# Gated delta rule in a three-way mixer: early preparation, a smaller last doubling, and query work moved later

## The reference, cut to what matters

```python
proj = rms_norm(h, norm_mix_pre[l]) @ w_in[l]
(aq, ak, av, cb, cc, cx, gq, gk, gv, ga, gb, gg) = jnp.split(proj, split_idx, axis=-1)
# delta rule, per head and chunk
rel = jnp.exp(jnp.where(causal, decay[..., :, None] - decay[..., None, :], -jnp.inf))
a = jnp.where(strict, jnp.einsum('bhnik,bhnjk->bhnij', k_beta, k) * rel, 0.0)
sol = lax.linalg.triangular_solve(eye + a, rhs, left_side=True, lower=True, unit_diagonal=True)
attn = jnp.where(causal, jnp.einsum('bhnik,bhnjk->bhnij', q, k) * rel, 0.0)
q_dec = q * jnp.exp(decay)[..., None]
def step(state, inp):
    v_new = u_i - jnp.einsum('bhck,bhkv->bhcv', w_i, state)
    o_i = einsum(q_i, state) + einsum(attn_i, v_new)
    state = state * cd_i[..., None, None] + jnp.einsum('bhck,bhcv->bhkv', k_i, v_new)
# then rms_norm(o, norm_w) * silu(gate), concatenated with the other two parts, @ w_out
```

## Time and profile before

| | us |
|---|---|
| median of 3 runs (2716.85 to 2727.89) | 2717.04 |
| the profiled execution | 2713.73 |
| its span, first to last instruction | 2711.9 |
| TensorE busy in the span | 2573.2 (95%) |
| VectorE busy | 1681.6 (62%) |
| ScalarE busy | 1136.8 (42%) |
| mean granted clock of TensorE | 0.976 |

### The profile page before, as it was taken

How to read it: one execution, slowest core, us unless ns; L and a number is a source line. 1 busy time by engine, 2 the same in 40 slices (tenths; PEclk the granted TensorE clock), 3 DMA queues, 4 the chain that set the end, 5 groups by cost and what they waited for, 6 DMA issues and landing times.

```text
span 2711.9 us, 34553 instructions
## 1 busy us (share of the span) xinstructions
PE 2573.2 (95%) x13186; PEld 2055.0 (76%) x13186; DVE 1681.6 (62%) x3253; ACT 1136.8 (42%) x2073; POOL 0.2 (0%) x4
## 2 busy tenths in 40 slices
PE   7998999899999999988999999999999999999897
PEld 5876879678888878668886788888876667787566
DVE  6756546455446776565564554468477676599664
ACT  4235444443232242454444433223345677232563
POOL 0000000000000000000000000000000000000000
PEclk9989999999999999899999999999899999999999
DMA  4310024123335622100331232375110000122221
GB/s 146 104 60 19 1 87 139 39 78 101 96 99 202 194 74 98 57 10 1 109 124 48 78 98 96 95 239 191 45 47 24 17 17 17 62 78 78 59 58 48
DMA packets 73507, 219.37 MB, mean 81 GB/s; under 512 B 21248, under 2 KB 21504, under 8 KB 72576
## 3 DMA queue, kind: packets, MB, share of 16 engines
q1 hardware_dynamic: 48384, 176.29, 20.1%
q10 hardware_dynamic: 24960, 40.87, 4.9%
HBM read 215.03 MB, written 2.10 MB: 80 GB/s over the span
## 4 chain that ended last, share of the span: by engine, by line
PE 80%; DVE 12%; ACT 5%; issue 2%; DMA 1%; ACTq 0%; DVEq 0%; SPq 0%
PE bank L575 20%; PE bank L576 19%; PE bank L577 19%; PE bank L842 4%; PE bank L806 4%; DVE c_y L2150 3%; PE bank L816 3%; DVE w_lo L541 2%; PE bank L1297 1%; PE bank L1305 1%; PE bank L606 1%; ACT w_hi L534 1%; PE bank L608 1%; PE bank L607 1%; PE bank L1243 1%
## 5 line engine op out<-in xcount | busy, mean ns | idle before, releaser
L575 PE MATMUL bank<-a_hi,w_hi 128*128 128x512 f32 (+1 forms) x1480 | 587.4, 397 | 25.4 <-DVE a_lo L712 16.0
L534 ACT ACTIVATE w_hi<-w_raw 128x1024 fp32r<-128x1024 f32 x334 | 353.0, 1060 | 570.3 <-PE bank L577 539.8
L576 PE MATMUL bank<-a_lo,w_hi 128*128 128x512 f32 (+1 forms) x1480 | 579.0, 391 | 0.0
L577 PE MATMUL bank<-a_hi,w_lo 128*128 128x512 f32 (+1 forms) x1480 | 579.0, 391 | 0.0
L541 DVE TENSOR_TENSOR w_lo<-w_raw,w_hi 128x1024 fp32r<-128x1024 f32 x334 | 407.7, 1223 | 232.8 <-ACT w_hi L534 232.1
L575 PEld LDWEIGHTS bank<-a_hi,w_hi 128*128 128x128 f32 (+1 forms) x1480 | 278.1, 188 | 97.3 <-issue 32.1
L576 PEld LDWEIGHTS bank<-a_lo,w_hi 128*128 128x128 f32 (+1 forms) x1480 | 278.0, 188 | 61.2 <-issue 3.0
L577 PEld LDWEIGHTS bank<-a_hi,w_lo 128*128 128x128 f32 (+1 forms) x1480 | 278.0, 188 | 60.8
L575 PE MATMUL bank<-b_hi,w_hi 128*128 128x512 f32 x704 | 258.4, 367 | 1.0 <-DVE w_lo L541 0.8
L576 PE MATMUL bank<-b_lo,w_hi 128*128 128x512 f32 x704 | 249.8, 355 | 0.0
L577 PE MATMUL bank<-b_hi,w_lo 128*128 128x512 f32 x704 | 248.3, 353 | 0.0
(11 more groups left out here) (399 smaller groups left out, 4019.6 us busy)
## 6 DMA issues: line engine op xcount, KB each, us to landing
w_raw<-w_tiles SPq DMA_DIRECT2D x334, 512.0 KB, 3.5
mod_raw<-mod_tiles ACTq DMA_DIRECT2D x48, 512.0 KB, 4.2
d_bias<-rpb_rows ACTq DMA_DIRECT2D x16, 224.0 KB, 4.5
hT<-xT ACTq DMA_DIRECT2D x4, 512.0 KB, 11.0
m_in<-memT ACTq DMA_DIRECT2D x2, 1024.0 KB, 4.7
mod_cond<-cond_rows ACTq DMA_DIRECT2D x2, 1024.0 KB, 6.2
out<-hT ACTq DMA_DIRECT2D x8, 256.0 KB, 2.6
ctx_sq<-ctxT ACTq DMA_DIRECT2D x1, 1024.0 KB, 7.7
```

Source lines behind the costliest of these rows:

```text
L534: act.activation(w_hi[:, t % SPLIT, :], w_raw[:, t % RAW, :], ACT.Copy).then_inc(sem("w_rounded"), 1)
L575: pe.matmul(o, wh, hi[:, k, :n], start=k == 0, stop=False)
L576: pe.matmul(o, wh, lo[:, k, :n], start=False, stop=False)
L577: mm = pe.matmul(o, wl, hi[:, k, :n], start=False, stop=k == kc - 1)
```

## The change

It does the following; no arithmetic of the result is left out.
- Preparation is interleaved with the input jobs: l2 sums and the turning of a and b after job ak0, two swaps after aq1, two swaps and the decay sums after cg0, the values' turning after cx0. VectorE's and ScalarE's parts are set one or more jobs behind (`in_between_*`). Each square follows the SiLU it needs. The loading of the count mask is issued at aq0.
- The gate's blocks in attention go 2, 3, 3, 4, 3, 3, 4, 4, 3, 3 over ten rounds in place of 4 in each of eight. The last gate's take on VectorE stands behind attention.
- The second short convolution is spread over attention units 2 to 6 on VectorE.
- Chunk 0 of the chunk loop is issued by TensorE in attention's last round, ahead of the last values' products; its exp of decay rows and the next diagonal stand on ScalarE ahead of the copy of these values.
- k x q is copied out of its bank by ScalarE, between the copies of k and v. Its product with rel and the decayed q are made by VectorE in doubling steps 2 to 5, one chunk in each.
- SiLU of the four gates is made in doubling steps 1 to 4. The four splits follow the output of each chunk in the recurrence; on VectorE they stand behind the gated result of the chunk before.
- Doubling step 6 changes only the upper right 64x64 block of each head's 128x128 matrix, so level, update and the turn before them are made on 64x64 blocks.

```diff
+        def in_between_pe(pe, l, name):
+            if name == "ak0":
+                gdn_first_pe(pe, l)
+            if name == "aq1":
+                swaps_pe(pe, l, 0)
+            if name == "cg0":
+                swaps_pe(pe, l, 1)
+                gdn_decay_pe(pe, l)
+            if name == "cx0":
+                values_turned_pe(pe, l)
+        GATE_BLOCKS = [2, 3, 3, 4, 3, 3, 4, 4, 3, 3]
@@ attention_pe
                 if fill:
                     for _ in range(blocks(i)):
                         next(fill, None)
+                if last and i == len(steps) + ahead:
+                    last()
                 if pending is not None:
                     att_values_pe(pe, key, units, group_of(units, pending), pt, vt)
@@ att_between_act
+                gate_split_act(act, l, u)
+                if u == after:
+                    decay_act(act, l, 0)
+                    diag_act(act, l, 1)
@@ gdn_pe, update
-                    mm = pe.matmul(head(b, h), head(yv[:, n, :], h), head(xt_inv[:, n, :], h),
+                    y = head(yv[:, n, :], h)
+                    if s == 6:
+                        mm = pe.matmul(b[UPPER, HALF * h:HALF * h + HALF], y[LOWER, 0:HALF],
+                                       head(xt_inv[:, n, :], h)[LOWER, HALF:P], start=True, stop=True)
@@ gdn_act
                 op.then_inc(*freed("kt", l, n, also=("kdec", l, n)))
+                b = bank(act, "kq", l, n)
+                act.activation(attn_t[:, n, :], b[:, :], ACT.Copy).then_inc(*freed("kq", l, n, also=("kq_in", l, n)))
                 b = bank(act, "vt", l, n)
...
+                if s <= GH:
+                    gate_act(act, l, s - 1)
             act.wait_ge(*when("att_out", l, AH // 2 - 1, 1))
-            act.wait_ge(*when("short", l, 1))
-            for c in range(4):
-                split_act(act, tmp[:, c, :], c, ("out", l))
             for n in range(TT):
...
+                split_act(act, tmp[:, n, :], n, ("out", l))
@@ gdn_dve
-                b = bank(dve, "kq", l, n)
-                dve.tensor_tensor(attn_t[:, n, :], rel_t[:, n, :], b[:, :], ALU.mult)\
-                   .then_inc(*freed("kq", l, n, also=("attn", l, n)))
...
+            def queries(n):
+                dve.wait_ge(*when("kq_in", l, n))
+                dve.tensor_tensor(attn_t[:, n, :], attn_t[:, n, :], rel_t[:, n, :], ALU.mult)\
+                   .then_inc(*done("attn", l, n))
+                x = by_head(0, n)
+                dve.tensor_tensor(x, x, dec[:, n, :].rearrange("p (h n) -> p h n", h=GH), ALU.mult)\
+                   .then_inc(*done("q_dec", l, n))
             for s in range(1, 7):
+                if 2 <= s < 2 + TT:
+                    queries(s - 2)
...
-            for c in range(4):
-                split_dve(dve, tmp[:, c, :], c, ("out", l))
...
                 if n:
                     out_gated_dve(dve, l, n - 1)
+                    split_dve(dve, tmp[:, n - 1, :], n - 1, ("out", l))
             out_diag_dve(dve, l, TT - 1)
+            split_dve(dve, tmp[:, TT - 1, :], TT - 1, ("out", l))
             out_gated_dve(dve, l, TT - 1)
```

More of the change, by code:

```diff
@@ L854, in lanes_of, with attention_pe @@
             return 1 + max(unit["lane"] for unit in units)
-        def attention_pe(pe, key, units, s, pt, vt, need=(), fill=None, blocks=None, need_at=None):
+        def attention_pe(pe, key, units, s, pt, vt, need=(), fill=None, blocks=None, need_at=None, last=None):
             for event in need:
@@ L1094, in short_conv_dve @@
                .then_inc(*done("short_in", l, c))
+            yield
             dve.wait_ge(*when("short_in", l, c))
@@ L1107, in short_conv_dve, with att_between_dve, between @@
             dve.tensor_tensor(tmp[:, 2 + c, :], cv_in[:, 2, :], y, ALU.mult).then_inc(*done("short", l, c))
+            yield
+        def att_between_dve(dve, l):
+            short = short_conv_steps(dve, l, 1)
+            def between(u):
+                gate_take_dve(dve, l, u)
+                if u >= 2:
+                    next(short, None)
+            return between
         def job_done_by(i):
@@ new lines, in gdn_chunk_pe @@
+        def gdn_chunk_pe(pe, l, n):
+            if n == 0:
+                pe.wait_ge(*when("silu", l, len(GDN) - 1))
+            tok = slice(P * n, P * n + P)
+            for w in range(2):
+                pe.wait_ge(*when("diag_decay" if w == 0 else "diag_beta", l, n))
+                b = claim(pe, "row", l, n, w)
+                pe.matmul(b[:, :], ones, (spread if w == 0 else sqacc)[:, :], start=True, stop=True)\
+                  .then_inc(*filled("row", l, n, w))
+            b = claim(pe, "kk", l, n)
+            for h in range(GH):
+                k = g_qkv[:, 3 * h + 1, tok]
+                mm = pe.matmul(head(b, h), k, k, start=True, stop=True)
+            mm.then_inc(*filled("kk", l, n))
+            b = claim(pe, "kq", l, n)
+            for h in range(GH):
+                mm = pe.matmul(head(b, h), g_qkv[:, 3 * h + 1, tok], g_qkv[:, 3 * h, tok], start=True, stop=True)
+            mm.then_inc(*filled("kq", l, n))
+            for name, j in (("kt", 1), ("vt", 2)):
+                b = claim(pe, name, l, n)
+                for h in range(GH):
+                    mm = pe.transpose(head(b, h), g_qkv[:, 3 * h + j, tok], ident)
+                mm.then_inc(*filled(name, l, n))
@@ L1285, in turn @@
+        def gdn_pe(pe, l):
+            for n in range(1, TT):
+                gdn_chunk_pe(pe, l, n)
             def turn(s, n):
@@ L1530, in gdn_dve @@
                                      op1=ALU.mult).then_inc(*done("neg_beta_exp_d", l))
[L1532 to L1538 removed]
+        def gdn_dve(dve, l):
             def relative(n):
```

236 lines of the change are left out of this document (134 added, 102 removed).

## The result

| | before | changed |
|---|---|---|
| median, measured together (us) | 2724.87 (2716.85 to 2727.89) | 2698.69 (2693.91 to 2706.86) |
| profiled execution (us) | 2713.73 | 2698.30 |
| its span (us) | 2711.9 | 2696.5 |
| granted clock | 0.976 | 0.976 |

The ratio is 0.9915, with a 95% interval of 0.9899 to 0.9931: about 23 us faster (19 to 28). The pair of profiled executions shows only 15.4 us, since the one of before happened to be faster than nearly all the timed ones.

The account below looks back on a forecast made before the run. TensorE, 80% of the span, was taken to bound the kernel. The terms summed to -12.8 us a layer, -25.6 in two: 2713.7 to 2688.1, plus 3.3 to the median, 2691.4 us; 8-in-10 range 2672 to 2707.

Parts of the forecast that it names:

- Preparation: Before attention: early sums and swaps remove TensorE idle time, -4.6 us a layer; their clock loss shrinks, -1.0.
- Attention: Regrouped gate products fill TensorE's end gaps, -3.8 us a layer; without gaps the clock stays up, -2.7.
- a gate take: In attention: 0.35 us of the 4.15 us gap left, since the first values meet VectorE's take of a gate.
- Chunk loop: Three-engine cycle from exp to exp lengthened to 7.0 us by the k x q copy: +2.5, less 0.6, +1.9 a layer.
- gaps of 2 us or more before k x q: Sign of being right: TensorE waits this long in the chunk loop, with exp to exp at 7.0 us.
- Doublings: 64x64 last step -4.0 us a layer; a later gap of 0.6 vanishes; query products moved here cost 0.
- small matmuls gain nothing: Rival on the 64x64 last doubling step: fixed time or drains eat its gain, 8 us worse, 2699; chance 0.13.
- 0.6 of latency: In the 64x64 last doubling step: 0.6 us of the 4.6 gain returns as VectorE and ScalarE steps are less covered.
- Recurrence: First v gap shrinks, -1.65 us; splits behind gated delay two right-hand sides and last output sum, +1.85; net +0.2 a layer.
- Clock later: Longer, emptier chunk loop adds clock loss beyond the recurrence's present 2.7 us: +1.2 us a layer.
- a clock below 0.9 in chunk loop or recurrence: Sign of being wrong: TensorE's granted clock under this level in either of the two stages.
- slower by the clock: Rival: chunk loop and recurrence run at the low clock throughout, +25 us a layer, 2742; chance 0.04.

Follow-up runs that it names:

- the second pair: Both kernels unaltered, profiled a second time: span 2720.3 us for the kernel before, 2701.1 us for the changed kernel.
- Experiment 6: Changed kernel with all preparation except the squares set back behind the last input product: 2710.2 us, ratio to before 0.9950.
- Experiment 1: Changed kernel with VectorE's take and the split of gate 0 moved from attention unit 6 to unit 4: 2690.48 us, ratio to before 0.9869.
- experiment 8: Changed kernel with four further edits (2673.36 us), its k x q copy now moved behind the v copy: 2673.91 us, ratio to before 0.9807.
- experiment 2: Changed kernel with the query products back on VectorE in the chunk loop and no ScalarE copy of k x q: 2699.31 us, ratio to before 0.9910.
- experiment 4: Changed kernel with doubling step 6 and the turn before it on 128x128 blocks again: 2714.51 us, ratio to before 0.9958.
- Experiment 5: Changed kernel with VectorE's splits in the recurrence moved from behind the gated result to ahead of the state's update: 2695.18 us, ratio to before 0.9896.

## Why the prediction was right, point by point

The time fell where it was forecast (2698.7 against 2691.4, within the range), but as a sum with one wrong term and one better than put. That the total came so near is partly luck. Attention alone fell 10.7 us short in two layers, preparation gave 3.4 back, and the stages of the profiled pair come to -15.4 us (the spans of the second pair differ by 19.2), against -25.6 forecast and -23 timed. The 4 to 8 us between the traces and the timed runs, whose interval is 19 to 28, lie in no row that I have.

- **Preparation (-4.6 and -1.0; measured -7.0 and -7.6).** Right, but 1.4 and 2.0 too small. The rows show no wait at the squares in the changed kernel and no gap ahead of the first scores at 175.06, so the 4.6 of gaps is gone. The clock was down 3.4 us less at the sums (10.2 for 13.7), which at half speed is 1.7 where 1.0 was put. The other 0.7 and 1.3 stay open. Experiment 6 gives back 3.3 in layer 0, once what lies ahead of the edit is taken off, and 2.9 in layer 1.
- **Attention (-3.8 and -2.7; measured -1.1 and -1.2).** This step failed. The old gap of 4.15 us did go, as argued. The 0.35 us left for "a gate take" was the mistake: I looked at the takes beside the values, not at the bank of the first one, whose next user is the fourth step's scores. With 2, 3, 3 blocks gate 0 ends in the third step, where its take lies behind two further units' VectorE work and the short convolution's steps, which I had put at 0 by their stage's idle share. The wait is 3.10 us, and the clock falls within it, so the -2.7 went too. Experiment 1 brings 5.3 a layer back. A stage's idle share doesn't say what stands ahead of the one instruction that frees a bank.
- **Chunk loop (+1.9 after the 0.6; measured +3.7 and +3.0 with its clock).** Its direction, its mechanism and its places hold: first exp 9.68 us behind the last turn (10.05 forecast), k x k behind L1665 in chunk 1, ring of 6.71 (7.0). Mis-sized: chunk 1's ring, 9.75 against 7.6 forecast, with the clock at its lower level in 6.8 us of it; and the k x q copy, which costs the ring 0.2 of its 0.55 us (experiment 8). The sign "gaps of 2 us or more before k x q" came only half: 1.44 us in chunk 2 and 2.07 in chunk 3. By experiment 2, moving the query products back gains 1.3 in the loop and costs 0.8 in the doublings, so of this part of the change next to nothing is left on balance.
- **Doublings (-4.0, the later gap's -0.6, and 0 for the query products).** The stage shows -4.1, against 4.6. Of this 3.3 belongs to the 64x64 step (experiment 4) and 0.64 is the gap at 260.84, which went as forecast and comes back when the query products return to the chunk loop (0.63, experiment 2). The rival "small matmuls gain nothing" falls. The 4.0 was too much by the turns and by the changes of form, as experiment 4 shows; the 0.6 of latency in it was not there.
- **Recurrence (-1.65 +1.85).** Every row came out: the first gap 2.34 to 0.73, the right-hand sides' 0.99 to 1.60 and 1.53, the last sum's +0.6. Experiment 5 takes the second term back. Layer 0's +1.7 goes with a clock of 0.87 (0.92 in the earlier trace rows); layer 1's is 0.0.
- **Clock later (+1.2).** Its sum is near, and its place is the chunk loop's 0.90 and the recurrence's 0.87. The sign of being wrong, "a clock below 0.9 in chunk loop or recurrence", did come in the recurrence, where before was at 0.92 already; in layer 0 that stage is 1.5 us longer than its +0.2, in layer 1 not at all, so the sign came without the forecast failing by it. The rival "slower by the clock" wanted half of both stages at the lower level; 6.8 us at a time came.
- **Between spans and medians** I took 3.3 us; the profiled execution of before was itself some 11 us below the median measured beside it. The 2717.04 that the forecast started from is also 7.8 below that median. That moved the absolute time, and the ratio not: forecast 0.9906 (2688.1 / 2713.7), measured 0.9915.

## What to carry to other kernels

When fills are regrouped among steps, follow each fill's bank to its next user and see how much stands ahead of the reader in its own queue; a stage's mean idle time doesn't answer that. In a ring of three engines, what counts is the order on the engine that closes it: issuing the next turn's first instruction ahead of this turn's last copies gained 3.6 us a layer, taking a copy off that engine (and giving its work to another in the loop) 1.3. Keep tiny matmuls apart: here a single sum between dense products left the clock at 1.00, and eight in a row brought it down for themselves and for what followed.

## What the runs showed of the hardware

- The clock fell without any idle time: 24.00 of 24 us busy, granted clock 0.79, with 64 one-column passes in a row; with the same products set eight passes at a time between dense ones 62.00 of 62 us ran at 1.00. Before the change the same sums stood behind a gap of 1.82 us, so that this cause could not be told from idling.
- A matmul pass of 64x64 in float32 follows the last at 0.058 us, one of 128x128 at 0.112. A change between the two forms cost 0.1 us: eight 128x128 passes between 64x64 groups took 1.09 us, not 0.89.
- Executions of one and the same kernel differed by 8.4 us in span (2711.9, 2720.3), with 9.8 us more at the lower clock level in the longer one (140.4 against 130.6).
